# Three more stages of a hybrid backbone as seven products of halves instead of eight

## The chip, the cores and the metric

The kernel runs on one core of a Trainium2 chip. The metric is the device time of one execution in microseconds. All arithmetic is float32.

## What is computed

Two trunk layers over 512 tokens (256 of context, 256 latent) of width 1024, then a final norm:

```python
for i in range(2):
    h = rms_norm(x, norm_mix[i]) * (1 + scale1) + shift1        # scale, shift, gate from the modulation
    y = even_mixer(h) if i == 0 else odd_mixer(h)               # ends in: concat(heads) @ w_out  (2048 x 1024)
    x = x + gate1 * y
    h = rms_norm(x, norm_ffn[i]) * (1 + scale2) + shift2
    x = x + gate2 * ((silu(h @ w1) * (h @ w3)) @ w2)
return rms_norm(x, final_norm)                                  # latents alone
```

The even mixer is Mamba-2 SSD heads beside GLA heads; the odd one is a gated delta rule (GDN) whose queries, keys and values come from `silu(conv5(h @ w_qkv))`, 4096 channels. After layer 1's mixer only the latents are needed.

## The kernel before

The program is written engine by engine; the order on each engine is the order in the code, and semaphores join them. Activations lie transposed, 128 channels on the partitions and tokens along the free axis. Weights come in blocks of 1 MB (8 chunks of 128 rows, 256 columns) into a ring of three slots on SyncE's queue; a slot is refilled when its block's last product has been made. There is no planner beyond the list of blocks in `make_plan`.

Stages in order: modulation, `xbc` projection and convolution, SSD scan, GLA scan, output projection `out0`, `ffn0`, `qkv` projection and convolution with `z1`, GDN scan, output projection `out1`, `ffn1`.

- `gemm` (L876) makes two tiles of 128 output channels from one or two blocks: 8 or 16 matmuls of 512 (or 256) columns per tile into one PSUM bank each. `gemm_and_norm` runs the four groups of an output projection with it. It puts two `norm_sum`s (the squares of a finished tile times a matrix of ones, accumulated in bank 5) behind each group from the second on and four at the end; `gla_transposes` or `gdn_transposes` stand in the first group.
- `up` in `ffn` already uses a form with seven products: weights, tokens and results are cut in two halves each way (2 x 2 blocks), and 7 products of 4 chunks by 256 columns replace 8, named p1 to p7. The sums of the weight halves (four operations of 512 columns per block) and of the token halves are made on VectorE, and the results are put together from copies by ScalarE (`first_copy` and so on) and adds by VectorE. `down` does the same for the last product with chunks paired over the inner dimension; its 7 products accumulate over three blocks per group of two tiles, and VectorE merges them in `down_taken`.
- `conv_stage` runs 16 groups of two tiles for `qkv`. Groups 0 to 3 are queries of the latents alone (256 columns), groups 4 to 15 have 512. ScalarE copies each tile into `raw`, VectorE makes the five taps into `conv` (one multiplication, four multiply-adds, L2326 and L2323), ScalarE applies SiLU. Tiles 16 to 31 are transposed on TensorE (L1074) and moved out by VectorE, and from group 9 on TensorE makes two L2 sums per group.
- `late_columns` and `mod1_columns` turn a row of modulation values into columns with four matmuls of two columns (matrix `pick`); VectorE adds the bias.
- GpSimd (L2956) has masks and decays of the scans, nothing during `out0`, the feed-forward layers and `qkv`.
- `keep_clock` issues four filler matmuls while the norm is scaled.

Matmuls all have line L815 in the profile, VectorE's adds L2320, multiply-adds L2323, copies L2329, ScalarE's operations L1777.

## Time and profile before

| | us |
|---|---|
| median of 3 runs (1952.24 to 1958.18) | 1953.9 |
| the profiled execution | 1957.48 |
| its span | 1955.7 |
| TensorE busy | 1888.6 (97%) |
| VectorE busy | 984.7 (50%) |
| ScalarE busy | 580.8 (30%) |
| GpSimd busy | 102.8 (5%) |

The span is the time from the first to the last instruction of the profiled execution; 1.8 us lie around it. A float32 matmul leaves two records in the trace, so "x16" is eight matmuls. The ends of matmuls are modelled and overlap the next start by 0.1 to 0.2 us: the step from start to start is the time that counts. In the timeline's rows the first number is the start from the span's beginning, the second the length of the merged row, and the bracket is idle time of that engine ahead of it with who ended it.

### The profile page before, as it was taken

To read this page: it belongs to the slowest core of one execution; us is meant where nothing else is said; L and a number is where in the kernel's file an instruction comes from. 1 tells how busy PE (TensorE), PEld (TensorE's weight loads), DVE (VectorE), ACT (ScalarE), POOL (GpSimd) and SP (SyncE) were. 2 spreads that over 40 slices of the span, in tenths; PEclk is the share of its full clock that TensorE was granted. 3 is DMA by queue.
4 is the path that set the end of the run, shared out by engine and by line. 5 is a ranking of instruction groups with operands and counts; after the bars stand their busy time and mean duration, and the time that the engine had idled before them with its cause. 6 is when DMAs were issued, how large, how long until landed. Compare 5 with 4: busy or idle time off the path is not lost.

```text
span 1955.7 us, 32367 instructions
## 1 busy us (share of the span) xinstructions
PE 1888.6 (97%) x13388; PEld 1344.3 (69%) x13388; DVE 984.7 (50%) x2002; ACT 580.8 (30%) x1340; POOL 102.8 (5%) x102
## 2 busy tenths in 40 slices
PE   6999999999999999999999999999989998999997
PEld 2444677776664448888888874445666666889997
DVE  2551576202782043445532365556857777056764
ACT  4121223522551021111100041224355777022210
POOL 0000231000000000000000000001211111000000
PEclk9999999999999999999999999999989999999999
DMA  7433101133301212222222231212224201344442
GB/s 293 172 123 135 73 22 44 65 151 124 137 3 43 97 63 76 92 90 90 86 76 81 70 124 65 79 65 73 87 88 174 88 2 66 115 144 165 159 163 97
DMA packets 28016, 193.71 MB, mean 99 GB/s; under 512 B 3004, under 2 KB 4285, under 8 KB 5854
## 3 DMA queue, kind: packets, MB, share of 16 engines
q1 hardware_dynamic: 27826, 191.51, 27.0%
q8 instruction: 106, 1.74, 0.4%
q14 instruction: 40, 0.33, 0.1%
q10 hardware_dynamic: 44, 0.14, 0.0%
HBM read 190.59 MB, written 1.05 MB: 98 GB/s over the span
## 4 chain that ended last, share of the span: by engine, by line
PE 89%; DVE 5%; ACT 3%; issue 1%; DMA 1%; POOL 0%; SPq 0%; ACTq 0%; DVEq 0%; POOLq 0%
PE psum L815 88%; DVE ws_sb L2320 2%; DVE gl_tmp_sb L2320 1%; ACT ws_sb L1777 1%; ACT arena_sb L1777 1%; DMA arena_sb<-w 1%; DVE ws_sb L2323 1%; ACT wide_sb L1777 0%; PE psum L1074 0%; DVE xT_sb L2323 0%; PE psum L1223 0%; ACT const_sb L1777 0%; PE psum L1234 0%; DVE ws_sb L2800 0%; DVE ws_sb L2801 0%
## 5 line engine op out<-in xcount | busy, mean ns | idle before, releaser
L815 PE MATMUL psum<-hT_sb,ring_sb 128*128 128x512 f32 (+3 forms) x1600 | 487.6, 456 | 1.1 <-ACT hT_sb L1777 1.1
L815 PEld LDWEIGHTS psum<-hT_sb,ring_sb 128*128 128x128 f32 (+1 forms) x1600 | 277.3, 189 | 194.3 <-issue 178.4
L1777 ACT ACTIVATE ws_sb<-psum 128x256 f32<-128x256 f32 (+5 forms) x373 | 164.6, 443 | 786.8 <-PE psum L815 775.5
L815 PE MATMUL psum<-arena_sb,ws_sb 128*128 128x256 f32 (+3 forms) x2064 | 345.1, 319 | 1.7 <-DVE hT_sb L2320 0.9
L815 PEld LDWEIGHTS psum<-arena_sb,ws_sb 128*128 128x128 f32 (+1 forms) x2064 | 289.7, 182 | 37.2 <-issue 12.7
L815 PE MATMUL psum<-arena_sb,ring_sb 128*128 128x256 f32 (+2 forms) x1200 | 293.9, 397 | 3.1 <-ACT arena_sb L1777 1.7
L815 PEld LDWEIGHTS psum<-arena_sb,ring_sb 128*128 128x128 f32 x1200 | 205.0, 192 | 83.5 <-issue 61.7
L815 PE MATMUL psum<-ring_sb,hT_sb 128*128 128x256 f32 (+3 forms) x1248 | 240.6, 372 | 0.1
L815 PEld LDWEIGHTS psum<-ring_sb,hT_sb 128*128 128x128 f32 (+1 forms) x1248 | 194.1, 176 | 52.9 <-issue 21.2
L2320 DVE TENSOR_TENSOR ws_sb<-ws_sb,psum 128x256 f32<-128x256 f32 (+2 forms) x218 | 87.6, 408 | 131.4 <-ACT ws_sb L1777 71.4
L2320 DVE TENSOR_TENSOR ws_sb<-ring_sb 128x512 f32<-128x512 f32 x132 | 89.2, 676 | 84.0 <-PE psum L815 80.0
L2323 DVE SCALAR_TENSOR_TENSOR ws_sb<-ws_sb,cols_sb 128x512 f32<-128x512 f32 (+1 forms) x176 | 123.7, 703 | 6.3
L2323 DVE SCALAR_TENSOR_TENSOR xT_sb<-psum,mod_sb,xT_sb 128x256 f32<-128x256 f32 x24 | 11.6, 484 | 162.5 <-PE psum L815 162.2
L815 PE MATMUL psum<-const_sb,arena_sb 64*128 64x256 f32 (+5 forms) x576 | 84.9, 394 | 5.1 <-ACT ws_sb L1777 2.0
L1777 ACT ACTIVATE arena_sb<-psum 128x512 f32<-128x512 f32 x56 | 33.5, 598 | 183.9 <-PE psum L815 182.7
L2956 POOL TENSOR_TENSOR wide_sb<-small_sb,const_sb 128x512 f32<-128x512 f32 x24 | 25.9, 1079 | 1106.7 <-DVE arena_sb L2329 1045.3
L1777 ACT ACTIVATE wide_sb<-xT_sb 128x512 f32<-128x512 f32 (+1 forms) x40 | 21.8, 545 | 198.5 <-PE psum L815 126.0
L815 PE MATMUL psum<-wide_sb,const_sb 128*32 128x256 f32 (+2 forms) x384 | 72.4, 447 | 7.4 <-ACT wide_sb L1777 3.2
L815 PEld LDWEIGHTS psum<-const_sb,arena_sb 64*128 64x128 f32 (+3 forms) x576 | 45.9, 177 | 41.5 <-issue 26.7
L2320 DVE TENSOR_TENSOR arena_sb<-ws_sb 128x256 f32<-128x256 f32 (+1 forms) x84 | 30.1, 358 | 86.5 <-ACT ws_sb L1777 85.1
L815 PE MATMUL psum<-ws_sb 128*32 128x32 f32 (+4 forms) x1872 | 65.4, 214 | 0.6 <-issue 0.6
L815 PE MATMUL psum<-hT_sb,ws_sb 128*128 128x256 f32 (+1 forms) x336 | 62.1, 328 | 1.0 <-ACT ws_sb L1777 1.0
(191 smaller groups left out, 1869.7 us busy)
## 6 DMA issues: line engine op xcount, KB each, us to landing
ring_sb<-w SPq DMA_DIRECT2D x146, 1024.0 KB, 4.8
hT_sb<-w SPq DMA_DIRECT2D x16, 1024.0 KB, 4.8
arena_sb<-w SPq DMA_DIRECT2D x8, 1024.0 KB, 19.0
ring_sb<-w SPq DMA_DIRECT2D x8, 768.0 KB, 4.0
xT_sb<-x SPq DMA_DIRECT2D x1, 2048.0 KB, 9.8
const_sb<-consts SPq DMA_DIRECT2D x1, 2048.0 KB, 10.5
y<-xT_sb SPq DMA_DIRECT2D x1, 1024.0 KB, 4.8
ring_sb<-w SPq DMA_DIRECT2D x2, 256.0 KB, 4.0
```

What stands on the lines that cost most here:

```text
L815: return nc.tensor.matmul(o, l, r, start=start, stop=stop, **kw)
L1777: return nc.scalar.activation(o, i, func, **kw)
L2320: return V.tensor_tensor(o, a, b, op)
L2323: return V.scalar_tensor_tensor(out=o, in0=a, scalar=sc, in1=b, op0=op0, op1=op1)
L2956: return G_.tensor_tensor(o, a, b, ALU.mult)
```

## The change

- `out0` and `out1` become `downs("out0", ...)` and `downs("out1", ...)`: the paired seven-product form. Each of the two halves of the mixed channels (SSD and GLA heads, or the first and last GDN heads) is one block per group, with chunks c and c + 4 as a pair. In the first group the products stand in another order, those with plain operands first.
- Groups 4 to 15 of `qkv` become units of `sevens("qkv")`. The results are put together in `raw`, so the taps of a unit's first tile come after the copy of p3, and those of its second tile after the add that follows p4. Before, the taps waited for one copy of a finished bank.
- GpSimd makes the weight sums of `qkv`'s units, its token sums, the first block's sums of both output projections and the token sums of the SSD half (all in `arena`, `ws` and `extra`).
- The squares of tiles 1 to 5 of four norms are added up by GpSimd in `wide[2]`; TensorE makes three sums at the end (`norm_total`).
- The modulation columns are made by transposes, and VectorE reduces the rows (`four_rows`).
- `ffn`'s two forms are the same as before, under other names.

```diff
+SEVENS = {"up0": (PLAIN[0], FC), "qkv": (4, 16), "up1": (PLAIN[1], FC)}
+DOWN_PAIRS = {"out0": (4, 4), "dn0": (4, 4, HALF_FC - 8), "out1": (4, 4), "dn1": (4, 4, HALF_FC - 8)}
...
+        SEVEN_BANKS = {"up0": ((4, 6), 5, 7), "qkv": ((0, 2), 1, 3), "up1": ((4, 6), 5, 7)}
+        LATENTS_ONLY = {"up0": 0, "qkv": 0, "up1": 1}
-                    last = mm(psum[:, 5, 2 * t:2 * t + 2], late_row[:, t * P:(t + 1) * P], cm("pick")[:, 0:2])
+                    last = nc.tensor.transpose(psum[:, 5, t * P:(t + 1) * P], late_row[:, t * P:(t + 1) * P], ident)
...
+            def norm_total(tag):
+                lo = NORMS[tag][2] * CTX
+                pe.wait_ge(S["square_used"], NORM_AT[tag][0] * KC + KC - 3)
+                mm(psum[:, 5, lo:T], ones, wide[:, 2, lo:T], start=True, stop=False).then_inc(S["square_used"], 1)
+                for c in (KC - 2, KC - 1):
+                    pe.wait_ge(S["square"], NORM_AT[tag][0] * KC + c + 1)
+                    mm(psum[:, 5, lo:T], ones, wide[:, c % 2, lo:T], start=False, stop=(c == KC - 1)).then_inc(S["square_used"], 1)
...
-            def gemm_and_norm(stage, src, total, tag, meanwhile=None):
...
+                if first < end:
+                    for g in range(max(first - 2, 0), first):
+                        for f in range(2):
+                            drained(pe, out_of(stage, g, f))
+                    sevens(stage, turned)
+                    pe.wait_ge(U["copies"], COPY["far", stage, end - 1])
+                    pe.wait_ge(U["adds"], ADD["up_near", stage, end - 1])
...
+                    if g == 0 and stage.startswith("out"):
+                        def side_ready(n):
+                            if part == 0:
+                                pe.wait_ge(U["sides"], SIDES_AT[stage] + n)
+                            else:
+                                pe.wait_ge(W["paired"], PAIRED_AT[stage] + 4)
+                        product(b0, 0, True, raw_weights(0, 0), lambda q: tokens(q, 0, 0))
+                        product(b3, b3_at // CTX, True, raw_weights(1, 0), lambda q: tokens(q, 1, 0))
+                        pe.wait_ge(W["sums"], DOWN_AT[stage] + k + 1)
+                        product(b2, 0, True, summed(4), lambda q: tokens(q, 1, 1))
+                        side_ready(1)
+                        product(b1, 1, True, summed(1), side(0))
+                        side_ready(2)
+                        product(b0, 1, False, summed(2), side(1)).then_inc(W["products"], 1)
+                        side_ready(3)
+                        product(b1, 0, False, summed(3), lambda q: tokens(q, 0, 1)).then_inc(W["products"], 1)
+                        side_ready(4)
+                        product(b2, 1, False, raw_weights(1, 1), side(2)).then_inc(W["products"], 2)
+                    else:
...
+                    if k == 0 and meanwhile:
+                        meanwhile()
+                norm_total(tag)
                 if tag != "fin":
...
+                for g in range(first, end):
+                    second_copied(stage, g)
+                    if g > first:
+                        activate(2 * g - 2)
+                    fourth_copied(stage, g)
+                    activate(2 * g - 1)
+                    besides(2 * g)
+                    if g + 1 < end:
+                        first_copied(stage, g + 1)
+                    act.wait_ge(U["products"], PRODUCT["p3", stage, g])
+                    act.wait_ge(C["conv"], 2 * g - 1)
+                    own(f(raw_halves(0)[1], half_width(psum[:, unit_bank(stage, g), :], 0), ACT.Copy).then_inc(U["copies"], 1), U["copies"])
+                    besides(2 * g + 1)
+                if first < end:
...
+            def four_rows(bank):
+                return psum[:, bank, :].rearrange("p (t c r) -> p t r c", c=4, r=32)[:, :, 0:2, :]
             def late_taken(q):
                 at = 4 * (MOD_FIRST + q)
                 dve.wait_ge(S["late_columns"], q + 1)
-                own(tt(mod[:, 0, at:at + 4], psum[:, 5, 0:8].rearrange("p (a b) -> p a b", b=2),
-                       bc(cl("mod_b", at, 4), 2, 2), ALU.add).then_inc(S["late_taken"], 1), S["late_taken"])
+                m = mod[:, 0, at:at + 4]
+                link(V.tensor_reduce(m, four_rows(5), AX_X, ALU.add))
+                own(tt(m, m, bc(cl("mod_b", at, 4), 2, 2), ALU.add).then_inc(S["late_taken"], 1), S["late_taken"])
...
+                for g in range(first, end):
+                    near_bank, far_bank = SEVEN_BANKS[stage][2], SEVEN_BANKS[stage][1]
+                    one, two, four = (half_width(a, 0) for a in SEVEN_HOMES[stage][2])
+                    dve.wait_ge(U["products"], PRODUCT["p2", stage, g])
+                    dve.wait_ge(U["copies"], COPY["p1", stage, g])
+                    own(tt(raw_halves(0)[0], one, half_width(psum[:, near_bank, :], 0), ALU.add).then_inc(U["adds"], 1), U["adds"])
+                    dve.wait_ge(U["products"], PRODUCT["p7", stage, g])
+                    dve.wait_ge(U["copies"], COPY["u4", stage, g])
+                    own(tt(raw_halves(1)[1], four, half_width(psum[:, far_bank, :], 0), ALU.add).then_inc(U["adds"], 1), U["adds"])
+                    if stage == "qkv" and g >= 10:
+                        l2_taken(g - 10)
+                    dve.wait_ge(U["copies"], COPY["far", stage, g])
+                    taps(2 * g)
+                    besides(2 * g)
+                    dve.wait_ge(U["products"], PRODUCT["p4", stage, g])
+                    own(tt(raw_halves(1)[0], two, half_width(psum[:, far_bank, :], 0), ALU.add).then_inc(U["adds"], 1), U["adds"])
+                    taps(2 * g + 1)
+                    besides(2 * g + 1)
                 if stage == "qkv":
                     l2_taken(6)
...
+            def out_begun(i):
+                stage = f"out{i}"
+                if i == 1:
+                    dve.wait_ge(S["mixed"], 20)
+                    halves_ = mixT1[:, 0:KC, :].rearrange("p (m c) (u l) -> p m u c l", m=2, l=P)
+                    b11, b12, b21, b22 = (halves_[:, m, u] for m in range(2) for u in range(2))
+                    t1, t2, t4 = (OUT_SIDES[1][0][n][:, :, 0:P] for n in range(3))
+                    for n, (o, x, y) in enumerate(((t1, b12, b11), (t2, b22, t1), (b12, b22, b12), (t4, b21, t2))):
+                        tt(o, x, y, ALU.subtract).then_inc(U["sides"], 1)
+                        dve.wait_ge(U["sides"], SIDES_AT[stage] + n + 1)
+                down_added_weights(stage, 1)
+                for q in range(4, 8):
+                    dve.wait_ge(S["mixed"], (8 + q + 1, 16 + (8 + q % 4 + 4) // 2 + 1)[i])
+                    pair_sums(stage, q)
+                downs(stage, 2)
...
+            def norm_squares(tag):
+                n, lo = NORM_AT[tag][0], NORMS[tag][2] * CTX
+                for c in range(1, KC - 2):
+                    pool.wait_ge(S["square"], n * KC + c + 1)
+                    G_.tensor_tensor(wide[:, 2, lo:T], wide[:, 2, lo:T], wide[:, c % 2, lo:T], ALU.add).then_inc(S["square_used"], 1)
+                    pool.wait_ge(S["square_used"], n * KC + c)
...
+            def first_out_weights(stage):
+                block, pairs, at, a = down_block(stage, 0)
+                s1, s2, s3, s4 = (down_sums(stage, 0)[:, m, 0:pairs * P].rearrange("p (c n) -> p c n", n=P) for m in range(4))
+                pool.wait_ge(s_w[(block - FIRST) % RING], 16 * ((block - FIRST) // RING + 1))
...
+                G_.tensor_tensor(s4, a[:, 1, :, 0, :], s2, ALU.subtract).then_inc(W["sums"], 1)
+                pool.wait_ge(W["sums"], DOWN_AT[stage] + 1)
+            def ssd_sums():
+                halves_ = mixT[:, 0:KC, :].rearrange("p (m c) (s u l) -> p m u c s l", m=2, u=2, l=P)
+                b11, b12, b21, b22 = (halves_[:, m, u] for m in range(2) for u in range(2))
+                t1, t2, t4 = (OUT_SIDES[0][0][n].rearrange("p c (s l) -> p c s l", l=P) for n in range(3))
+                for n, (o, x, y) in enumerate(((t1, b12, b11), (t2, b22, t1), (b12, b22, b12), (t4, b21, t2))):
+                    if n == 3:
+                        pool.wait_ge(S["gla_taken"], 16)
+                    G_.tensor_tensor(o, x, y, ALU.subtract).then_inc(U["sides"], 1)
+                    pool.wait_ge(U["sides"], SIDES_AT["out0"] + n + 1)
...
+            def added_weights(stage):
+                first, end = SEVENS[stage]
+                for j in range(first, end):
+                    block, a = unit_weights(stage, j)
+                    s1, s2, s3, s4 = (unit_sums(stage, j)[:, m, :].rearrange("p (c n) -> p c n", n=P) for m in range(4))
+                    pool.wait_ge(s_w[(block - FIRST) % RING], 16 * ((block - FIRST) // RING + 1))
+                    if j > first + 1:
+                        pool.wait_ge(U["products"], PRODUCT["p4", stage, j - 2])
...
+                    G_.tensor_tensor(s4, a[:, 1, :, 0, :], s2, ALU.subtract).then_inc(U["sums"], 1)
+                    pool.wait_ge(U["sums"], unit_no(stage, j) + 1)
+            pool.wait_ge(S["mixed"], 8)
+            pool.wait_ge(S["gla_lv"], 48)
+            first_out_weights("out0")
+            ssd_sums()
+            norm_squares("ffn0")
+            norm_squares("mix1")
+            token_sums("qkv", "mix1")
+            added_weights("qkv")
             pool.wait_ge(S["beta_lanes"], 1)
             pool.wait_ge(s_masks, 16)
             pool.wait_ge(S["edge"], 2)
             pool.wait_ge(conv_sems["qkv"]["tr_taken"], 16)
             gdn()
...
+            pool.wait_ge(G["sd"], 28)
+            first_out_weights("out1")
+            norm_squares("ffn1")
+            norm_squares("fin")
```

On TensorE, in groups 12 and 13 of `qkv`: `ring_sb` holds weights, `ws_sb` and `extra_sb` weight sums after, `const_sb` the identity or ones, `hT_sb` the normed tokens, `arena_sb` their sums. Before:

```order
L815 MATMUL psum<-hT_sb,ring_sb 128x512 x16
L1074 MATMUL psum<-const_sb,ws_sb 128x128 x8
L815 MATMUL psum<-wide_sb,const_sb 128x512 x2
L815 MATMUL psum<-hT_sb,ring_sb 128x512 x16
L1074 MATMUL psum<-const_sb,ws_sb 128x128 x8
```

After:

```order
L880 MATMUL psum<-wide_sb,const_sb 128x512 x2
L880 MATMUL psum<-arena_sb,ws_sb 128x256 x8
L880 MATMUL psum<-hT_sb,ring_sb 128x256 x4
L880 MATMUL psum<-arena_sb,ws_sb 128x256 x4
L880 MATMUL psum<-hT_sb,ring_sb 128x256 x4
L880 MATMUL psum<-hT_sb,ws_sb 128x256 x4
L880 MATMUL psum<-arena_sb,ring_sb 128x256 x4
L1148 MATMUL psum<-const_sb,ws_sb 128x128 x8
```

One group's 16 matmuls of 512 columns became 28 of 256; the transposes and L2 sums stay between the units.

On VectorE, two tiles of `qkv` from tile 20 on (`cols_sb` holds the tap weights). Before:

```order
L2326 TENSOR_SCALAR ws_sb<-ws_sb,cols_sb 128x512
L2323 SCALAR_TENSOR_TENSOR ws_sb<-ws_sb,cols_sb 128x512 x4
L2329 COPY arena_sb<-psum 128x4x128
L2326 TENSOR_SCALAR ws_sb<-ws_sb,cols_sb 128x512
L2323 SCALAR_TENSOR_TENSOR ws_sb<-ws_sb,cols_sb 128x512 x4
L2329 COPY arena_sb<-psum 128x512 x2
```

After:

```order
L2456 TENSOR_TENSOR ws_sb<-ws_sb,psum 128x2x128 x2
L2465 COPY arena_sb<-psum 128x512 x2
L2462 TENSOR_SCALAR ws_sb<-ws_sb,cols_sb 128x512
L2459 SCALAR_TENSOR_TENSOR ws_sb<-ws_sb,cols_sb 128x512 x4
L2465 COPY arena_sb<-psum 128x4x128
L2456 TENSOR_TENSOR ws_sb<-ws_sb,psum 128x2x128
L2462 TENSOR_SCALAR ws_sb<-ws_sb,cols_sb 128x512
L2459 SCALAR_TENSOR_TENSOR ws_sb<-ws_sb,cols_sb 128x512 x4
```

Two adds stand ahead of the first tile's taps now, and one between the two tiles' taps.

On GpSimd, between the SSD scan (the 32 operations) and the GDN scan (the two behind them) nothing stood before:

```order
L2950 UNCONDITIONAL_BRANCH
L2956 ISA
L2956 TENSOR_TENSOR ws_sb<-small_sb,const_sb 128x512 x32
L2956 TENSOR_TENSOR wide_sb<-small_sb,const_sb 128x512 x2
L2981 MEMSET ws_sb 128x1024
```

After, part of what stands there:

```order
L3239 TENSOR_TENSOR arena_sb<-ring_sb,arena_sb 128x512
L3250 TENSOR_TENSOR arena_sb<-arena_sb 128x1024 x2
L3250 TENSOR_TENSOR arena_sb<-arena_sb 128x8x128
L3250 TENSOR_TENSOR arena_sb<-arena_sb 128x1024
L3143 TENSOR_TENSOR wide_sb<-wide_sb 128x512 x10
L3225 TENSOR_TENSOR arena_sb<-hT_sb 128x1024
```

The weight sums of the first block and the SSD half's token sums stand ahead of the norms' adds, and `qkv`'s sums follow.

## Rows read from the trace of the kernel before

**Rows 1.** The page: busy time; shares of the chain that ended last

```profile
PE 1888.6 (97%) x13388; PEld 1344.3 (69%) x13388; DVE 984.7 (50%) x2002; ACT 580.8 (30%) x1340; POOL 102.8 (5%) x102
...
PE 89%; DVE 5%; ACT 3%; issue 1%; DMA 1%; POOL 0%; SPq 0%; ACTq 0%; DVEq 0%; POOLq 0%
```

**Rows 2.** Timeline of TensorE, output projection 0

```profile
588.12 14.00 PE L815 MATMUL psum<-arena_sb,ring_sb 128*128 128x512 f32 x32 [0.85 <-DVE hT_sb L2320]
...
608.78 41.47 PE L815 MATMUL psum<-arena_sb,ring_sb 128*128 128x512 f32 x96 [0.84 <-ACT arena_sb L1777]
...
712.10 3.60 PE L815 MATMUL psum<-const_sb 128*128 128x512 f32 x8
```

**Rows 3.** Timeline of TensorE, feed-forward layers 0 and 1, two units each

```profile
801.91 1.89 PE L815 MATMUL psum<-arena_sb,ring_sb 128*128 128x256 f32 x8
...
814.00 1.89 PE L815 MATMUL psum<-arena_sb,ring_sb 128*128 128x256 f32 x8
...
1742.05 1.06 PE L815 MATMUL psum<-arena_sb,ring_sb 128*128 128x128 f32 x8
...
1748.30 1.06 PE L815 MATMUL psum<-arena_sb,ring_sb 128*128 128x128 f32 x8
```

**Rows 4.** Timeline of TensorE in qkv

```profile
1270.40 13.90 PE L815 MATMUL psum<-hT_sb,ring_sb 128*128 128x512 f32 x32
...
1284.14 1.04 PE L1074 MATMUL psum<-const_sb,ws_sb 128*128 128x128 f32 x8
...
1285.01 1.88 PE L815 MATMUL psum<-wide_sb,const_sb 128*128 128x512 f32 x4
...
1350.78 7.33 PE L815 MATMUL psum<-ring_sb,hT_sb 128*64 128x256 f32 x48
```

**Rows 5.** Timeline of ScalarE and VectorE in qkv; the page's adds with PSUM

```profile
1169.37 0.39 ACT L1777 ACTIVATE ws_sb<-psum 128x256 f32<-128x256 f32 x1 [0.51 <-PE psum L815]
...
1278.76 3.11 DVE L2323 SCALAR_TENSOR_TENSOR ws_sb<-ws_sb,cols_sb 128x512 f32<-128x512 f32 x4
...
L2320 DVE TENSOR_TENSOR ws_sb<-ws_sb,psum 128x256 f32<-128x256 f32 (+2 forms) x218 | 87.6, 408 | 131.4 <-ACT ws_sb L1777 71.4 <-PE psum L815 42.1 <-issue 15.1
```

**Rows 6.** Timeline of TensorE at the end of feed-forward layer 0

```profile
1123.53 1.12 PE L815 MATMUL psum<-wide_sb,const_sb 128*128 128x512 f32 x2 [1.25 <-ACT wide_sb L1777]
...
1125.86 3.60 PE L815 MATMUL psum<-const_sb 128*128 128x512 f32 x8
```

**Rows 7.** Timeline of TensorE, one turn of modulation columns in the GLA scan

```profile
489.11 0.95 PE L815 MATMUL psum<-const_sb,extra_sb 128*128 128x2 f32 x8
...
489.99 0.53 PE L815 MATMUL psum<-ws_sb 128*32 128x32 f32 x38
```

**Rows 8.** TensorE's timeline; windows: length, busy of five engines, clock, DMA

```profile
1661.48 8.80 PE L815 MATMUL psum<-arena_sb,ring_sb 128*128 128x256 f32 x32
...
1725.45 3.60 PE L815 MATMUL psum<-const_sb 128*128 128x512 f32 x8
...
1660.00:1663.00 3.00, 2.92 (x11) 2.21 (x10) 1.41 (x4) 1.83 (x3) 0.00 (x0) 0.50 0.01 3
```

**Rows 9.** Timeline of VectorE and GpSimd where both run

```profile
239.23 1.41 DVE L2320 TENSOR_TENSOR ws_sb<-ws_sb,small_sb 128x512 f32<-128x512 f32 x1
...
240.68 0.69 DVE L2320 TENSOR_TENSOR ws_sb<-ws_sb,psum 128x512 f32<-128x512 f32 x1
...
238.68 2.86 POOL L2956 TENSOR_TENSOR ws_sb<-small_sb,const_sb 128x512 f32<-128x512 f32 x2 [4.71 <-PE psum L815]
...
1379.02 2.16 POOL L2956 TENSOR_TENSOR wide_sb<-small_sb,const_sb 128x512 f32<-128x512 f32 x2 [8.85 <-PE psum L815]
...
1381.26 6.05 POOL L2956 TENSOR_TENSOR const_sb<-const_sb,ws_sb 128x256 f32<-128x256 f32 x8
```

**Rows 10.** Timeline of VectorE and TensorE at the end of the GLA scan

```profile
576.30 2.85 DVE L2320 TENSOR_TENSOR ws_sb<-ws_sb,arena_sb 128x256 f32<-128x256 f32 x8
...
582.39 0.67 PE L815 MATMUL psum<-arena_sb,ws_sb 128*128 128x256 f32 x2 [0.73 <-DVE ws_sb L2323]
```

523 lines of the change are left out of this document (296 added, 227 removed).

## The prediction

> **What bounds the kernel now.** I read the page first: TensorE is busy for 97% of the span, and the chain that ended last runs over TensorE for 89% [rows 1]. So time can be won by taking TensorE work away, unless another engine then ends a wait. Next I read TensorE's timeline stage by stage, in which each matmul has two records. A matmul of 512 columns costs 13.73/16 = 0.86 us (the step from 1270.40 to 1284.14 is one group of 16) [rows 4]. In the feed-forward layers of this same kernel, one unit of seven products (28 matmuls of 256 columns) repeats every 814.00 - 801.91 = 12.09 us, 0.432 us each, with no idle time, and every 6.25 us where the tokens are halved, 0.223 us per 128 columns [rows 3]. So the seven-product form can run at TensorE's pace. The question is whether it does in the three new places. For that I read VectorE, ScalarE and GpSimd there.
>
> **Output projection 0.** Before, it runs from 588.12 to 712.10 = 124.0 us [rows 2]: 128 matmuls of 512 columns (110.5), 6.8 for the transposes, from the end of the first 13.85 us of matmuls to 608.78, 4 norm sums inside (3.45), and 3.6 at the end. After: 8 blocks of 28 matmuls of 256 columns, 224 x 0.4316 = 96.7; the transposes stay (ScalarE's evictions pace them); the end is a chain add, residual, square, sum. The exit of the first feed-forward layer has that chain in the trace: the last product ends 1.25 us before 1123.53, at 1122.28, and the filler matmuls start at 1125.86, 3.6 us [rows 6]. The one extra sum (0.86), of what GpSimd added up, fits into those 1.25 us. Total 107.1, so **-16.9**. Cover: VectorE has four weight sums of 512 columns (each 0.69, like the 512-column add at 240.68 [rows 9]) per block of 12 us, and per group of 24 us ten operations of half a microsecond for the merging. The pair sums of chunks 4 to 7 (four times 4 operations of 0.42 [rows 5]) start as the transposes end; TensorE has three products (5.2 us) before it needs them, so I price them at nothing, and at 1 us in the range.
>
> **Output projection 1.** Before 1661.48 to 1725.45 = 64.0 [rows 8]. After: 224 matmuls of 128 columns, 224 x 0.2233 = 50.0, transposes 3.0, end 2.2, and a stall I expect at the second block: four pair sums of about 1.2 us (4 operations of 128 columns) stand in a row on VectorE after the last heads are mixed, and TensorE has only 2.7 us of products ahead of them, 1.7 of stall. 56.9, so -7.1. GpSimd's four weight sums run beside VectorE's 16 operations that feed the transposes; I take 1.6 us for that, two and a half of the holds of 0.62 worked out below. **-5.5**.
>
> **Norms.** Each of the four norms drops from 8 sums on TensorE to 3. In the two projections that is counted above. In down 0, six sums of 0.86 stand inside the stage (two are 1.72 us, as from 1285.01 on [rows 4]): **-5.2**. In down 1 half of it: **-2.6**. The adds move to GpSimd (5 of 1.04 us) long before the end; nobody waits.
>
> **Modulation columns.** Four matmuls of two columns (8 records) step 489.99 - 489.11 = 0.88 us [rows 7]; four transposes are half of the eight that step 1285.01 - 1284.14 = 0.87 [rows 4], 0.44. 20 places: 8 in the first projection (-3.5, TensorE is gapless there), 4 in the GLA scan and 8 in the gated-delta scan (-5.2 at most). VectorE gains a small reduction each time (0.2 us), and those scans have waits on VectorE, so I take -4.0 for the 12. **-7.5**.
>
> **The convolution groups**, the place that decides. Before, groups 4 to 8 take 13.73 us each, groups 9 to 12 16.33 (plus transposes 0.87 and L2 sums 1.73) [rows 4]; all 12 run from 1169.0 (tile 7, the last before them, was copied at 1169.37 [rows 5]) to 1350.78 = 181.7. Products alone would fall by 12 x (13.73 - 12.09) = 19.7 us. But the loop is longer here than in the feed-forward layer. Per unit VectorE must do: the two adds, then after the last ScalarE copy the five taps of the first tile (four in 3.11, the first about 0.55 ahead of them, 3.66), an eviction (about 0.7, from group 9 on), and only then the add that frees TensorE's bank for the next unit's p7, then the second tile's taps [rows 5]. The loop is: five products from p7 to p3 (8.64), ScalarE's copy of 0.39 and both hand-overs (0.8), taps 3.66, an add of 0.41 and its hand-over (0.6): **13.7 us**, against 12.09 for the products. So even undisturbed units 4 to 8 gain nothing; from group 9 on the 2.6 us of transposes and sums cover the difference partly (14.7 against 16.3). Stepping through the twelve units with these durations gives 177 us in place of 181.7.
>
> Then the weight sums. They are on GpSimd, which starts them when p4 of the unit before ends, 2 us into those taps. What that does is in the trace [rows 9]: a VectorE add of 512 columns with both inputs in SBUF takes 1.41 us beside two GpSimd operations and these take 1.43 each, where alone two take 2.16; the next add, with one input in PSUM, takes 0.69 beside the same operations. So while both run they alternate. GpSimd's 512-column operation costs 1.08 and its 256-column one 0.76 (eight in 6.05), so 0.42 is fixed and 0.62 is what it holds; 0.69 + 0.62 is about the 1.41. The taps have both inputs in SBUF. Two to three of them lie in the window, so each unit's add is 1.3 to 1.9 us later: units of 15.0 (one hold of 0.62 per tap) to 16.2 (VectorE at half speed as long as GpSimd runs). The twelve give 189 to 200 us; the first is nearer the measured pair of 512-column operations, I take 191. At the entry TensorE now waits until tile 7 is copied, and that copy waits for the taps of tile 5 (before: copied at 1169.37, just in time [rows 5]), delayed by GpSimd's first two sets of sums: 2.7 us. Sum 191 + 2.7 - 181.7 = **+12**; bounds -4 (no sharing) and +21.
>
> The Trainium skill speaks against this placement: GPSIMD Engine Reference, section 8 "Key points", says that GpSimd shares its SBUF interfaces with VectorE and contends with VectorE instructions that have two SBUF inputs. By this rule the trace agrees: 1.41 against 0.69 us, and the operation with a PSUM input untouched.
>
> **The end of the GLA scan.** GpSimd now does the first block's sums and the first three of the SSD chunks' sums as soon as the last scores are made (about 575.6): 4 operations of 1.04 and three of 1024 columns, by the two sizes above 0.42 + 1.24 = 1.66 each, about 9 us in all. VectorE stands there in a row of eight 256-column operations (576.30, 2.85 us) on which the scan's last outputs depend, and TensorE already waits for VectorE at 582.39 and 588.12 [rows 2, 10]. Each GpSimd operation holds VectorE for 0.62 to 1.24: +2.5 if two of the eight pass per GpSimd operation, +6.7 if one does. I take +4, and +1 for the clock: at the same kind of place in front of projection 1, where TensorE waits at every transpose, the granted clock stood at 0.50 from 1660 to 1663 [rows 8], the 1.2 GHz level. **+5**.
>
> **Sum**: -16.9 - 5.5 - 5.2 - 2.6 - 7.5 + 12 + 5 = -20.7. The profiled execution took 1957.5 us (span 1955.7); 1936.8 for it. The median of the runs is 3.6 lower, 1953.9; I forecast **1934**.
>
> **Rivals.**
> 1. No sharing that matters (the taps take their gaps between GpSimd's operations, and the projections' early sums find VectorE idle). For: the row of tensor adds with PSUM input at 0.69. Against: [rows 9]. The three prices go: 12 to -4, 5 to 0, 1.6 to 0. Total -20.7 - 16 - 5 - 1.6 = -43, **1911**. Chance 0.13.
> 2. The sharing is heavier: GpSimd's sums of strided ring weights are slower than contiguous ones, or each tap waits for a whole GpSimd operation (1.04) and not for its hold. Units of 16.2, the groups +21, the scan's end +9: -20.7 + 9 + 4 = -8, **1946**. Chance 0.17.
> 3. The other side, slower: the tap loop. If each unit's five taps meet four full GpSimd operations (4 x 1.04 on top of 3.66), the loop is 17.9 us, and five units at 4.1 and seven at about 2 above before cost 35 us, 38 with the entry; with the scan's end at +9 the total is -37.7 + 38 + 9 = +9, **1963**. It decides from units of 16.8 us on. Against: GpSimd starts 2 us into the taps. Chance 0.08.
> 4. The seven products don't save what they should (weights not there in time, since blocks of 1 MB go every 6.2 us in projection 1): the feed-forward layer takes them as fast from the same three slots without a wait [rows 3], so it is unlikely; +4, **1938**. Chance 0.04.
>
> **How the numbers follow.** The forecast's case (1922 to 1945) has 0.58. A measurement tells about 0.3% (6 us). Faster by more than that is below 1948: the forecast, rival 1, and most of rival 2, 0.58 + 0.04 + 0.13 + 0.09 = 0.84, less 0.05 for what I did not see: 0.79. Same 0.11, slower 0.10. The range leaves a tenth at either side: 1913 to 1955.
>
> **What would show it.** In the profile after: projection 0 near 107 us and projection 1 near 57; seven-product units of the convolution at 15 to 16 us with TensorE waiting before p7 for VectorE's add, and taps of 1.3 to 1.5 us beside GpSimd; the scan's end some 4 us later with the same waits on VectorE; three norm sums at each exit. Wrong would be: units of 13.7 or less (rival 1), units over 16.8 (rival 3), or a wait of TensorE for the weight sums themselves.

## The result and the profile after

The changed kernel takes 1976.31 us (median of 4 runs, 1975.13 to 1978.93), the kernel before 1954.8 us beside it: a ratio of 1.011 (95% interval 1.009 to 1.013). It is slower by 1.1%, where I had forecast 1934 us, faster by 1%. The measured time lies outside the range of 1913 to 1955.

The page of the changed kernel, to be read against [rows 1]: span, busy times, shares of the chain that ended last by engine, and the group of matmuls that waits most (its idle time and who ended it stand at the end of the row).

```profile
span 1974.4 us, 33946 instructions
PE 1852.1 (94%) x13940; PEld 1432.7 (73%) x13940; DVE 1141.3 (58%) x2206; ACT 587.7 (30%) x1372; POOL 228.7 (12%) x186
PEclk9999999999989999999999988898989999899999
PE 29%; DVE 10%; ACT 2%; issue 1%; POOL 0%; DVEq 0%; ACTq 0%; POOLq 0%
L880 PE MATMUL psum<-arena_sb,ws_sb 128*128 128x256 f32 (+3 forms) x2208 | 387.7, 328 | 20.2 <-DVE ws_sb L2456 19.3
```

TensorE is busy for 36.5 us less, and its share of the span falls from 97 to 94%: the work went away, and more than that came back as waits. (The chain's shares add up to only 42% here, so nothing is read from them.) VectorE is busy for 1141 us where it was 985. Most of that is new work, the sums and adds of the seven-product form; but 34 us of it go when only the timing of GpSimd's sums is changed (1107.1 in the first experiment), so some of VectorE's instructions had become longer.

The timeline of TensorE in the changed kernel gives the starts of the stages: output projection 0, filler, filler, the first z product, output projection 1, filler, the last sum of squares.

```profile
592.03 3.72 PE L880 MATMUL psum<-arena_sb,ring_sb 128*128 128x256 f32 x16 [0.85 <-DVE hT_sb L2456]
...
699.10 3.60 PE L880 MATMUL psum<-const_sb 128*128 128x512 f32 x8
...
1107.71 3.60 PE L880 MATMUL psum<-const_sb 128*128 128x512 f32 x8
...
1379.28 9.01 PE L880 MATMUL psum<-ring_sb,hT_sb 128*64 128x256 f32 x48 [3.46 <-issue]
...
1689.38 2.48 PE L880 MATMUL psum<-arena_sb,ring_sb 128*128 128x128 f32 x16
...
1746.99 3.60 PE L880 MATMUL psum<-const_sb 128*128 128x512 f32 x8
```

With the starts of before that makes this table (the first stretch ends where VectorE begins its last row of eight products in the GLA scan, 576.30 before and 568.22 after):

| stretch | before, us | after, us | change | forecast |
|---|---|---|---|---|
| start to the last eight products of the GLA scan [rows 10] | 576.30 | 568.22 | -8.1 | about -5 (columns) |
| to output projection 0 [rows 2] | 11.82 | 23.81 | +12.0 | +5 |
| output projection 0 [rows 2] | 123.98 | 107.07 | -16.9 | -16.9 |
| feed-forward layer 0 [rows 6] | 413.76 | 408.61 | -5.2 | -5.2 |
| queries, convolution units [rows 4] | 224.92 | 271.57 | **+46.7** | +12 |
| gated-delta scan [rows 8] | 310.70 | 310.10 | -0.6 | -1 (columns less sharing) |
| output projection 1 [rows 8] | 63.97 | 57.61 | -6.4 | -7.1 |
| feed-forward layer 1 and the end | 230.25 | 227.41 | -2.8 | -2.6 |

The first stretch is not as sharp as it looks. The code ahead of this row of eight is the same in the changed kernel and in all the kernels below, and in their twelve traces the row starts between 568.22 and 572.77 us, 3.5 to 8.1 earlier than before. The changed kernel's trace is the earliest of them.

What the change removes from TensorE in the projections and norms came within 1 us of its price. Two stretches swallowed it, the convolution units above all. One unit there, in the timeline of VectorE, GpSimd and TensorE (changed kernel, p6 to p2 of unit 7, with the taps of unit 6):

```profile
1209.92 0.49 DVE L2462 TENSOR_SCALAR ws_sb<-ws_sb,cols_sb 128x512 f32<-128x512 f32 x1 [2.69 <-ACT ws_sb L1880]
1210.45 5.97 DVE L2459 SCALAR_TENSOR_TENSOR ws_sb<-ws_sb,cols_sb 128x512 f32<-128x512 f32 x4
1216.45 0.42 DVE L2456 TENSOR_TENSOR ws_sb<-ws_sb,psum 128x256 f32<-128x256 f32 x1
1216.91 0.92 DVE L2462 TENSOR_SCALAR ws_sb<-ws_sb,cols_sb 128x512 f32<-128x512 f32 x1
...
1211.26 1.27 POOL L3262 TENSOR_TENSOR extra_sb<-ring_sb 128x512 f32<-128x512 f32 x1 [11.87 <-PE psum L880]
1212.61 1.59 POOL L3263 TENSOR_TENSOR extra_sb<-extra_sb,ring_sb 128x512 f32<-128x512 f32 x1
1214.28 1.59 POOL L3264 TENSOR_TENSOR extra_sb<-ring_sb 128x512 f32<-128x512 f32 x1
1215.83 1.72 POOL L3265 TENSOR_TENSOR extra_sb<-ring_sb,extra_sb 128x512 f32<-128x512 f32 x1
...
1210.92 1.89 PE L880 MATMUL psum<-arena_sb,ws_sb 128*128 128x256 f32 x8
1216.92 3.78 PE L880 MATMUL psum<-arena_sb,ws_sb 128*128 128x256 f32 x8 [4.11 <-DVE ws_sb L2456]
1220.50 3.03 PE L880 MATMUL psum<-hT_sb,ring_sb 128*128 128x256 f32 x8
```

Read it in this order. VectorE's four multiply-adds take 5.97 us, where the same four take 3.11 in the kernel before [rows 5]. GpSimd's four weight sums run beside them: they start 0.8 us behind the first multiply-add (1211.26) and end at 1217.55, beside the add and the next multiplication. VectorE's add (1216.45) comes behind the taps, and p7 needs the bank that it frees: TensorE waits 4.11 us. Then p7 takes 3.78 us in place of 1.89, and p2 3.03: TensorE runs at half its clock after the wait (granted clock 0.50 from 1216.9 to 1220.4). Units 5 to 9 take 18.15 and 19.36 us by turns.

The other stretch, the end of the GLA scan (VectorE, GpSimd and TensorE, changed kernel):

```profile
568.22 13.18 DVE L2456 TENSOR_TENSOR ws_sb<-ws_sb,arena_sb 128x256 f32<-128x256 f32 x8
...
567.76 1.28 POOL L3236 TENSOR_TENSOR arena_sb<-ring_sb 128x512 f32<-128x512 f32 x1 [255.43 <-PE psum L880]
...
573.42 7.36 POOL L3250 TENSOR_TENSOR arena_sb<-arena_sb 128x1024 f32<-128x1024 f32 x3
...
582.09 0.76 PE L880 MATMUL psum<-ws_sb 128*32 128x32 f32 x40 [10.90 <-DVE ws_sb L2456]
```

The eight products took 2.85 us before [rows 10]. Now seven GpSimd operations (four of 512 columns, three of 1024 at 2.45 us) lie beside them, and they take 13.18: about one VectorE operation passes for each of GpSimd's. These 10.3 us more, and 1.7 us behind them, where TensorE's granted clock is 0.70 (582 to 592), make the +12.0.

### The profile page after: what moved, and what is told of

Read it like the earlier page. It is cut to its first block and busy times, and to the rows that moved or that the text cites. A ratio compares the mean times of both kernels' runs of the same rounds, so it can differ in the third digit from the quotient of the medians.

```text
span 1974.4 us, 33946 instructions
## 1 busy us (share of the span) xinstructions
PE 1852.1 (94%) x13940; PEld 1432.7 (73%) x13940; DVE 1141.3 (58%) x2206; ACT 587.7 (30%) x1372; POOL 228.7 (12%) x186
## 5 line engine op out<-in xcount | busy, mean ns | idle before, releaser
L880 PE MATMUL psum<-arena_sb,ws_sb 128*128 128x256 f32 (+3 forms) x2208 | 387.7, 328 | 20.2 <-DVE ws_sb L2456 19.3
L880 PE MATMUL psum<-hT_sb,ring_sb 128*128 128x256 f32 (+3 forms) x1408 | 373.4, 414 | 7.9 <-ACT ws_sb L1880 6.7
L880 PEld LDWEIGHTS psum<-arena_sb,ws_sb 128*128 128x128 f32 (+1 forms) x2208 | 321.3, 185 | 63.7 <-DVE ws_sb L2456 21.7
L880 PEld LDWEIGHTS psum<-hT_sb,ring_sb 128*128 128x128 f32 (+1 forms) x1408 | 246.3, 193 | 118.4 <-issue 95.1
L880 PE MATMUL psum<-ring_sb,hT_sb 128*128 128x256 f32 (+3 forms) x1248 | 242.3, 375 | 3.6 <-issue 3.5
L2456 DVE TENSOR_TENSOR ws_sb<-ws_sb,psum 128x256 f32<-128x256 f32 (+2 forms) x310 | 121.2, 399 | 198.3 <-ACT ws_sb L1880 102.2
L880 PE MATMUL psum<-arena_sb,ring_sb 128*128 128x256 f32 (+1 forms) x1168 | 214.1, 333 | 3.0 <-ACT arena_sb L1880 1.7
L2459 DVE SCALAR_TENSOR_TENSOR ws_sb<-ws_sb,cols_sb 128x512 f32<-128x512 f32 (+1 forms) x176 | 157.7, 896 | 6.3
L880 PE MATMUL psum<-arena_sb 128*32 128x32 f32 (+2 forms) x1552 | 108.6, 246 | 1.0 <-DVE arena_sb L2456 1.0
L880 PEld LDWEIGHTS psum<-arena_sb 128*32 128x32 f32 (+1 forms) x1552 | 96.6, 141 | 10.4 <-DVE arena_sb L2456 1.2
L3130 POOL TENSOR_TENSOR ws_sb<-small_sb,const_sb 128x512 f32<-128x512 f32 x32 | 41.7, 1303 | 270.2 <-DVE small_sb L2459 152.8
## 6 DMA issues: line engine op xcount, KB each, us to landing
arena_sb<-w SPq DMA_DIRECT2D x8, 1024.0 KB, 16.9
const_sb<-consts SPq DMA_DIRECT2D x1, 2048.0 KB, 10.5
```

What stands on the lines that cost most here:

```text
L880: return nc.tensor.matmul(o, l, r, start=start, stop=stop, **kw)
L2456: return V.tensor_tensor(o, a, b, op)
L2459: return V.scalar_tensor_tensor(out=o, in0=a, scalar=sc, in1=b, op0=op0, op1=op1)
L3130: return G_.tensor_tensor(o, a, b, ALU.mult)
```

## The experiments

The theory (A) after this look: while GpSimd works, only one of VectorE's operations that read SBUF alone passes per GpSimd operation. That makes the loop from taps to add to p7 longer, TensorE waits, and a half clock after the wait adds to it. The rivals: the loop is that long by itself; the clock falls for another reason; the sums themselves come late. A ratio compares with the kernel before, run beside each set (medians of 1952.2 to 1954.8 us); where two kernels of different sets are compared, differences of some 2 us mean little, and the stage's length in the traces counts.

**GpSimd's sums at another time.** One wait on GpSimd:

```diff
-                    if j > first + 1:
-                        pool.wait_ge(U["products"], PRODUCT["p4", stage, j - 2])
+                    if j > first:
+                        pool.wait_ge(U["products"], PRODUCT["p7" if j == first + 1 else "p2", stage, j - 1])
```

> One wait changed: in the convolution groups GpSimd starts the weight sums of unit j when p2 of unit j-1 is done (in the changed kernel: when p4 of unit j-2 is done), so that they run while VectorE is idle between its two bursts of taps. VectorE's work and order are the same. Theory A (VectorE's operations with two SBUF inputs pass only one per GpSimd operation): four taps fall from 5.97 us to 3.1 to 3.5, the first tap to 0.49 everywhere, TensorE's wait ahead of p7 from 4.11 to 1.2 to 1.5 us, the wait at the entry (6.74) to 3.5 to 5; units of 13.5 to 15 us where they took 18.15 to 19.36, in all 38 to 55 us less: 1921 to 1938 us. Theory B (the loop copy, taps, add, product is that long by itself, GpSimd or not): waits ahead of p7 stay at 4 us, units at 18 to 19, 1976 us. Theory C (both the sharing and something later, the GpSimd sums themselves): the wait ahead of p7 goes but a wait for the sums ahead of p6 appears, 1 to 3 us a unit, 1940 to 1965 us.

Measured: 1939.9 us (1937.76 to 1941.2), ratio 0.993 (0.991 to 0.994). VectorE and GpSimd in one unit of this kernel, and TensorE's p7 in two:

```profile
1184.47 3.11 DVE L2459 SCALAR_TENSOR_TENSOR ws_sb<-ws_sb,cols_sb 128x512 f32<-128x512 f32 x4
...
1179.73 1.27 POOL L3263 TENSOR_TENSOR extra_sb<-extra_sb,ring_sb 128x512 f32<-128x512 f32 x1
...
1188.10 1.99 PE L880 MATMUL psum<-arena_sb,extra_sb 128*128 128x256 f32 x8 [1.25 <-DVE ws_sb L2456]
...
1201.70 1.99 PE L880 MATMUL psum<-arena_sb,ws_sb 128*128 128x256 f32 x8 [1.25 <-DVE ws_sb L2456]
```

The taps are back at 3.11 us with the same work on both engines, the wait is 1.25 us, p7 runs at full clock, and a unit takes 1201.70 - 1188.10 = 13.60 us. Theory A holds in each of these, and with 3.83 us for the wait at the entry; only the total is 2 us above its range; TensorE's waits in the last two units and ahead of the z products (5.27, 2.42 and 3.47 us) are left. The loop "by itself" (B) falls, and no wait ahead of p6 appears (C). The stage from filler to z takes 234.3 us, against 271.6: the collision in time cost 37.3 us, the half clock behind the waits included. It is not down to the 224.9 of before, though: 9.4 us remain.

**The clock's share.** Filler matmuls ahead of p7, into a bank that the next product overwrites:

```diff
                 def p7(j):
+                    if stage == "qkv" and j > first:
+                        pe.wait_ge(U["adds"], ADD["near", stage, j - 1])
+                        for _ in range(8 if j < 10 else 4):
+                            mm(psum[:, near_bank, :], ones, cms("ident", 4).rearrange("p a b -> p (a b)"))
```

> Filler matmuls of 512 columns stand ahead of p7 in the convolution units (eight in units 5 to 9, four in units 10 to 15; 0.45 us each), where TensorE waits 4.11 and 2.25 us for VectorE's add. Nothing else changes; they fill the wait and write a bank that the next product overwrites. If the granted clock falls because TensorE waits there (theory A), p7 takes 1.9 us in place of 3.35 to 3.78 and p2 1.9 in place of about 3.0, units 5 to 9 and 14 to 15 take 16.5 to 17 us in place of 18.2 to 20: 10 to 20 us less, 1956 to 1966. If the clock falls there for another reason (theory D: load on all engines), the products keep their lengths and the time stays at 1976, or rises by up to 3 where the filler is longer than the wait.

Measured: 1980.47 us (1979.84 to 1981.18), ratio 1.014 (1.012 to 1.015). The edit was mis-sized and settles little: eight matmuls leave 16 records and take 6.9 us, longer than the wait of 4.11. The products behind them did run at full length, but the filler's surplus ate that. So I cut it to four and two:

> The filler again, cut to fit into the waits: in the run before, one filler matmul left two records of 0.43 us (0.86 us in all), so eight took 6.9 us against a wait of 4.11. Now four ahead of p7 in units 5 to 9 (3.45 us, wait 4.11) and two in units 10 to 15 (1.7 us, wait 2.25). Theory A (a wait of TensorE of 4 us in every 18 brings the clock to half, the products behind it pay): p7 takes 1.9 us in place of 3.35 to 3.78, p2 1.9 in place of 3.0, units 5 to 9 take 16.3 to 16.6 us in place of 18.15 to 19.36; 12 to 18 us less in all, 1958 to 1964. Theory D (the clock falls there for a reason other than the wait): no gain, 1976.

Measured: 1965.7 us (median of five; four lie at 1963.85 to 1966.99, the fifth at 3377.88 and is out of the ratio), ratio 1.005 (1.003 to 1.007). TensorE in one unit, and then the windows of four units (length; busy times of five engines; clock; DMA) of this kernel:

```profile
1209.02 3.60 PE L880 MATMUL psum<-const_sb 128*128 128x512 f32 x8
1213.30 1.99 PE L880 MATMUL psum<-arena_sb,ws_sb 128*128 128x256 f32 x8 [0.68 <-DVE ws_sb L2460]
```

```profile
1180.40:1246.20 65.80, 63.12 (x256) 48.27 (x256) 46.13 (x52) 13.20 (x34) 24.44 (x17) 1.00 0.18 64
```

and the same four units in the changed kernel:

```profile
1179.50:1254.40 74.90, 58.48 (x224) 48.63 (x224) 46.11 (x52) 13.20 (x34) 24.44 (x17) 0.86 0.16 56
```

VectorE and GpSimd do the same in the same time (46.1 and 24.4 us), and VectorE's add ends the wait as late as ever. Only TensorE's clock differs, 1.00 against 0.86, and a unit takes 16.5 us against 18.7. So of those 18.7 us about 2.3 are the price of the half clock alone. Between 16.5 and the 13.6 of the run with later sums, 2.9 us are the sharing; the last 1.5 above the products' 12.09 are the loop. The units fall into theory A's range, the whole does not: the stage is 12.1 us shorter (259.5), but the gated-delta scan behind it is 2.0 us longer in this trace (312.1).

**VectorE's order.** The add that frees the bank ahead of the taps, GpSimd as in the changed kernel:

```diff
-                    dve.wait_ge(U["copies"], COPY["far", stage, g])
-                    taps(2 * g)
-                    besides(2 * g)
                     dve.wait_ge(U["products"], PRODUCT["p4", stage, g])
                     own(tt(raw_halves(1)[0], two, half_width(psum[:, far_bank, :], 0), ALU.add)...)
+                    dve.wait_ge(U["copies"], COPY["far", stage, g])
+                    taps(2 * g)
+                    besides(2 * g)
                     taps(2 * g + 1)
```

> Only VectorE's order in a convolution unit is changed: the add that frees the bank for the next p7 comes ahead of the first tile's taps (in the changed kernel behind them). GpSimd's sums start where they did, in the middle of the taps. Theory A (the wait is the loop copy, taps, add; the sharing only makes the taps long): the wait ahead of p7 goes entirely, though the taps still take 6 us for four; VectorE's work per unit is then 2 x 3.6 of taps, 1.7 of adds and about 2.9 of sharing, 11.8 us, just under the 12.1 of the products; units of 12.1 to 13.5, no wait ahead of the z products: 1918 to 1930. Theory E (VectorE's whole work, not the order, is what is late): the wait shows up ahead of p5 or p4 for the next adds, 1 to 3 us a unit, 1935 to 1950.

Measured: 1948.31 us (1944.48 to 1951.9), ratio 0.997 (0.995 to 0.998). TensorE in one unit, and VectorE's first taps and, one unit on, the add behind p4:

```profile
1214.05 1.99 PE L880 MATMUL psum<-hT_sb,ws_sb 128*128 128x256 f32 x8 [0.19 <-ACT ws_sb L1880]
1217.40 1.99 PE L880 MATMUL psum<-arena_sb,ring_sb 128*128 128x256 f32 x8 [1.36 <-DVE ws_sb L2456]
...
1206.98 5.78 DVE L2459 SCALAR_TENSOR_TENSOR ws_sb<-ws_sb,cols_sb 128x512 f32<-128x512 f32 x4
...
1219.50 0.42 DVE L2456 TENSOR_TENSOR ws_sb<-ws_sb,psum 128x256 f32<-128x256 f32 x1 [2.16 <-PE psum L880]
```

The wait ahead of p7 is gone, but one of 1.36 us stands ahead of p4, for the next add behind the taps, and the stage takes 242.3 us. So theory E names the right wait, and its total is right, but not its reason: VectorE idles too, 2.16 us in each unit of 14.2, for p4. The two wait for each other in a new loop: p4, the bank-freeing add, both tiles' taps (10.5 us, where they take 7.2 without the sharing), the two adds, p4 again. Order alone gives 29 us of the stage back, timing alone 37.

**Plain groups.** `SEVENS["qkv"] = (16, 16)`, no token or weight sums for them:

> The convolution groups go back to plain matmuls of 512 columns, all 16 groups as in the kernel before (GpSimd makes no token or weight sums for them). The rest of the change stays. By the stages of the two traces the convolution part cost 46.7 us: from filler to z products 271.6 back to 224 to 226 us, 1929 to 1931 us. If part of that loss came from elsewhere (norms, columns, a lower clock brought in from ahead), 1935 to 1950. If the stages around it had gained from a late convolution, below 1925.

Measured: 1930.01 us (1928.46 to 1931.87), ratio 0.988 (0.986 to 0.989). The stage takes 224.9 us, as before. So the whole 46.7 us were made inside it. (The row of eight started late in this trace, 572.77, and the gated-delta scan was 1.4 us shorter; other stages keep their lengths to 0.2 us, the end of the GLA scan to 0.6.)

**The end of the GLA scan.** GpSimd's early sums wait until VectorE has done its eight products:

```diff
-            pool.wait_ge(S["gla_lv"], 48)
+            pool.wait_ge(S["gla_qk"], 16)
```

> GpSimd's first weight sums and first three token sums of projection 0 wait until VectorE has done the last row of eight products of the GLA scan (in the changed kernel they start as the last scores' inputs are ready). Theory A (one VectorE operation with two SBUF inputs passes per GpSimd operation): the row of eight falls from 13.18 to 2.85 us, TensorE's wait of 10.90 us ahead of it to 2 or less, no half clock before the projection; projection 0 starts 9 to 12 us earlier, its own length grows by 0 to 3 us because the sums now meet VectorE's sixteen scalings: 1965 to 1970 us. Theory B (the row waits for something else): no change, 1976. Theory C (the sums come too late for the first block): TensorE waits for them at the start of projection 0, 3 to 6 us, 1970 to 1974.

Measured: 1966.69 us (1966.14 to 1968.79), against 1976.31; ratio 1.007 (1.005 to 1.008). VectorE's eight products, its sixteen scalings, and TensorE's start of projection 0:

```profile
570.28 2.85 DVE L2456 TENSOR_TENSOR ws_sb<-ws_sb,arena_sb 128x256 f32<-128x256 f32 x8
...
584.42 11.51 DVE L2459 SCALAR_TENSOR_TENSOR hT_sb<-hT_sb,small_sb,arena_sb 128x256 f32<-128x256 f32 x16 [0.75 <-ACT small_sb L1880]
...
582.10 3.72 PE L880 MATMUL psum<-arena_sb,ring_sb 128*128 128x256 f32 x16 [0.85 <-DVE hT_sb L2456]
```

The projection starts 11.8 us after the eight products began, as in the kernel before, where it was 23.8: theory A. The sharing has only moved: the sixteen scalings now take 11.51 us, where they took 8.76 in the changed kernel. But TensorE has 12 us of products there (582.10 to 594.29) that do not need them, and projection 0 keeps its 107.07 us. What a collision costs depends on who waits.

Both together:

> Plain convolution groups as in the earlier run, and GpSimd's early sums of projection 0 behind the GLA scan's last products: if the two costs are separate, 46.7 and 10 us come off 1976.3: 1919 to 1921. If the loss at the scan's end was paid back later (a wait that then moves), 1925 to 1930.

Measured: 1917.83 us (2 runs, 1915.92 and 1919.74), ratio 0.981 (0.977 to 0.984). The two costs add, as far as two runs can tell.

**The same at projection 1.** On top of that, GpSimd's first weight sums of projection 1 ahead of its last multiplications of the gated-delta scan, into 53 us of idle time:

```diff
+                pool.wait_ge(G["sd"], 28)
+                first_out_weights("out1")
                 pool.wait_ge(S["mix_rs"], 3)
```

> The fastest so far (plain convolution groups, GpSimd's early sums of projection 0 behind the GLA scan's last products), and the four weight sums of projection 1's first block moved on GpSimd ahead of its last eight multiplications of the gated-delta scan, into an idle time of 53 us, so that they no longer run beside VectorE's sixteen scalings. Theory A (sharing): the sixteen scalings fall from 10.15 to 6.4 us, as in the kernel before, and projection 1 begins 3 to 4 us earlier: 1913 to 1915 us. Theory H (TensorE waits there for ScalarE's evictions and the multiplications, not for the scalings): 1917 to 1918.

Measured: 1914.04 us (1912.52 to 1915.81), ratio 0.980 (0.978 to 0.982). VectorE's sixteen scalings take 6.41 us instead of 10.15, and TensorE starts projection 1 at 1629.24, 306.3 us after the z products, where it was 309.6. The scalings in the run before and in this one:

```profile
1623.14 10.15 DVE L2461 SCALAR_TENSOR_TENSOR hT_sb<-hT_sb,small_sb,arena_sb 128x128 f32<-128x128 f32 x16
...
1622.86 6.41 DVE L2461 SCALAR_TENSOR_TENSOR hT_sb<-hT_sb,small_sb,arena_sb 128x128 f32<-128x128 f32 x16
```

**Can the seven-product units pay at all?** First VectorE's new order and GpSimd's sums from the end of p5 of the unit before, with the GLA edit:

> Seven products kept in the convolution groups, with both costs taken out: VectorE's bank-freeing add ahead of the taps, GpSimd's sums from the end of p5 of the unit before (VectorE's second burst of taps ends about then), and GpSimd's early sums of projection 0 behind the GLA scan's last products. Theory A: units 5 to 8 of 12.1 to 12.5 us, units 9 to 13 of 14.7 (2.6 of transposes and sums of squares on top), one wait of 5 us left at unit 14, where ScalarE is busy for 10 us with the scales; 1908 to 1914 us. Theory F (GpSimd's sums, 5.1 us, starting 5.2 us ahead of the product that reads them, come late): a wait of 0.5 to 1.5 us ahead of p6 per unit with its price in clock, 1916 to 1930.

Measured: 1920.79 us (1919.1 to 1923.04), ratio 0.982 (0.980 to 0.985). TensorE ahead of p6 in two units of this kernel:

```profile
1185.89 3.72 PE L880 MATMUL psum<-arena_sb,ws_sb 128*128 128x256 f32 x16 [0.24 <-POOL ws_sb L3265]
...
1198.62 3.72 PE L880 MATMUL psum<-arena_sb,extra_sb 128*128 128x256 f32 x16 [0.38 <-POOL extra_sb L3265]
```

Theory F: a unit takes 12.6 to 12.7 us, and the sums come 0.2 to 0.6 us late. The stage takes 226.2 us, no better than plain groups. Then VectorE makes the weight sums itself, between its adds and the next taps; GpSimd keeps the stage's token sums, and projection 1's first sums are moved as above:

> Seven products in the convolution groups, the bank-freeing add ahead of the taps, and the unit's four weight sums on VectorE (4 x 0.7 us, between its adds and the next taps) instead of GpSimd; GpSimd's early sums of projections 0 and 1 moved as in the other runs. Theory A: nothing shares with VectorE any more; VectorE's unit is 7.2 + 1.7 + 2.8 = 11.7 us of the 12.1 of the products; units 5 to 8 take 12.1 us, the entry wait falls from 3.84 to 1 to 2.5 us, the wait of 5.8 us at unit 14 for ScalarE stays; 1908 to 1913 us. Theory G (with 11.7 of 12.1 us used, hand-overs make VectorE the bound): waits of 0.5 to 1.5 us per unit, 1915 to 1925.

Measured: 1914.07 us (1910.96 to 1915.24), ratio 0.980 (0.978 to 0.982). Units 5 to 13 run without a wait, at 12.09 us where nothing stands between them, and the stage takes 222.7 us. The entry's wait is 0.76 us in place of 6.74, but a new one follows it: TensorE waits 2.63 us ahead of the first p6, until VectorE has made the first unit's sums (VectorE ends them at 1147.89). The largest wait left is TensorE's for ScalarE, at unit 14, with the half clock behind it:

```profile
1148.00 6.90 PE L880 MATMUL psum<-arena_sb,extra_sb 128*128 128x256 f32 x24 [2.63 <-issue]
...
1291.92 3.78 PE L880 MATMUL psum<-arena_sb,extra_sb 128*128 128x256 f32 x8 [5.78 <-ACT ws_sb L1880]
```

ScalarE computes the scales of the keys there for 10 us, and had idled 2.66 us for TensorE just before, ahead of two squares. So the last run swaps the two:

```diff
-                    if stage == "qkv" and t >= 16 and t % 2 == 1:
-                        l2_squares(t // 2 - 8)
                     if stage == "qkv" and t == 27:
                         l2_scales(0)
+                    if stage == "qkv" and t >= 16 and t % 2 == 1:
+                        l2_squares(t // 2 - 8)
```

> The seven-product version of the run before with two ScalarE steps swapped at unit 13: the scales of the keys (two table loads and two functions over 4096 columns, 10 us) now stand ahead of the squares that wait 2.66 us for TensorE. Theory A: they begin 3.5 us earlier, TensorE's wait of 5.78 us at unit 14 falls to 2 to 2.5 us and less of what follows runs at half clock (p7 3.78 us there): 4 to 6 us less, 1908 to 1910 us, ahead of both kernels and of the plain groups. Theory J (the unit behind it has its own waits of 0.5, 3.5 and 2.4 us ahead of the z products, which absorb an earlier start): 1911 to 1914.

Measured: **1910.46 us** (1909.69 to 1911.67), ratio 0.978 (0.976 to 0.979): 2.2% faster than the kernel before, 3.3% faster than the changed one. The wait and p7 behind it:

```profile
1287.72 1.99 PE L880 MATMUL psum<-arena_sb,extra_sb 128*128 128x256 f32 x8 [3.21 <-ACT ws_sb L1880]
```

The wait is 3.21 us, above theory A's 2 to 2.5, and the total lies at the edge of its range. The stage takes 217.5 us, 5.2 less than in the run before. So in this stage the seven products are worth 7.4 us against plain groups, once nothing of GpSimd's weight sums collides. In the median the kernel is only 3.6 us ahead of the fastest one with plain groups (1914.04, another set of runs), and the gated-delta scan is 2.0 us shorter in that one's trace (306.3 against 308.3).

## Why the prediction was wrong

**What held.** The terms of the two projections and of the norms: -16.9, -5.2 and -2.8 as forecast, projection 1 -6.4 for -7.1. The modulation columns (7.5 us) can't be read so sharply, since no run takes them out alone: 3.5 to 8.1 us are gone by the end of the GLA scan (about 5 forecast), and the gated-delta scan is 2.3 to 4.4 us shorter where the sharing is out of it (308.4 and 306.3, before 310.7). The kind of mechanism was the right one: the taps, the add and the GpSimd sums beside them are what the prediction named. It named rival 3, the slower side, with its place and its point of decision (units over 16.8 us), and gave it 0.08. Units 5 to 9 took 18.2 to 19.4. But rival 3 had 17.9 us from four full GpSimd operations and no half clock; without the half clock they take 16.5 (the filler run), so its units come near the measured ones by a term that it did not have.

**The convolution term (+12 forecast, +46.7 measured)** was the sum of two parts, -4 without sharing and +16 for it. Both failed: the hold and the window were sized too small, the clock was priced at nothing, and ScalarE and the entry were left out of the loop without sharing.

*The size of a hold.* I took rows of other operations [rows 9] and made 0.62 us per GpSimd operation of them, the part above a fixed 0.42 (1.08 and 0.76 us give 0.64 and 0.44; the difference is small). But those are GpSimd operations with one or both inputs broadcast, and so is the one of 1.04 us. The sums have two full inputs, and such an operation takes 1.27 us alone and up to 1.72 beside VectorE. A kind with two full inputs and one with a broadcast input stand in the changed kernel's groups of instructions on GpSimd (count, busy time, mean ns of one), at the end of the gated-delta scan, and the kernel before had them there too:

```profile
L3130 POOL TENSOR_TENSOR hT_sb<-hT_sb,arena_sb 128x512 f32<-128x512 f32 x4 | 5.1, 1273 | 53.7 <-ACT small_sb L1880 53.4
L3130 POOL TENSOR_TENSOR hT_sb<-hT_sb,small_sb 128x512 f32<-128x512 f32 x4 | 4.2, 1041 | 0.3
```

In the taps four of them add 5.97 - 3.11 = 2.86 us to the multiply-adds and 0.43 to the next multiplication, 0.8 us each; at projection 1 four add 10.15 - 6.41 = 3.74, 0.9 each. And I had two to three of them in the window, since I let GpSimd start 2 us into the taps. It starts 1.3 us after the first (1211.26 against 1209.92), and above all the taps stretch under the sharing, so that all four fall in: a window worked out from undisturbed durations is too short.

*The clock.* I had a term for it at the GLA scan (+1), none in the units. The shorter filler run shows 2.3 us in each of the units 5 to 9, more than half as much as the wait itself. By filling the waits alone the stage went from 271.6 to 259.5, so some 12 of the 37.3 us are the clock's.

*The loop without sharing.* Units 5 to 8 are 13.6 us, by the forecast 13.7. But the stage is 9.4 us longer than before, not 4 shorter. I stepped through TensorE and VectorE and treated ScalarE as free: it holds 10 us of scales at unit 13, and copies of the next unit stand behind them (a wait of 5.27 us in the run with later sums). And I priced neither the wait for the last unit's second tile ahead of the z products (3.46 us) nor the half clock after such waits. The entry, too, was too small: I had 2.7 us with sharing and nothing without, and TensorE waits 6.74 and 3.83 us there, with part of the next 16 records at half clock.

37.3 us with sharing and its clock against the forecast's 16, and +9.4 against -4: that is the whole difference of 34.7 us.

**The end of the GLA scan (+5 forecast, +12)**: I wrote "+6.7 if one passes per GpSimd operation" (with my own holds it is 4 x 0.62 + 3 x 1.24 = 6.2) and took +4. One did pass. The operations of 1024 columns hold VectorE for about their whole length: the seven add 10.3 us, and at an assumed 0.9 for each of the four short ones, 2.2 remain for each long one, an estimate, where I had 1.24. The other 1.7 us of the stretch stand where the clock is at 0.70; I had 1. The Trainium skill names the kind in GPSIMD Engine Reference, section 8 "Key points" (shared SBUF interfaces, VectorE instructions with two SBUF inputs), and by it the trace agrees again: the adds with a PSUM input stay at 0.42 us beside GpSimd. The multiplication by a column has one tensor from SBUF and yet took 0.92 us in place of 0.49. The same sentence of the page also names VectorE instructions in a "2-port perf mode"; whether this multiplication is one, no run here shows.

**The range and the chances.** The bounds of the convolution term were -4 (no sharing) and +21 (units of 16.2 us). The upper one had no half clock in the units and no wait for ScalarE, and rival 3, above it, had neither. And hold, window and clock were priced apart, or not at all, while each makes the next larger.

What stays open: which property of the clock decides. After a wait of 4.11 us the next product ran at half, after 3.21 us (last run) and 2.27 us it did not, and after 3.47 us it did in the last run and not in the one before. In the changed kernel it did after 3.11 and 2.42 us too (units 14 and 15); with the sums of projection 0 moved, the same wait at unit 14 (3.12 us) left the clock full. The runs show the price, not the rule.
